# A decoder step on one core: modulation tiles placed one by one, the mLSTM update behind the numerator, and the RWKV-7 preparation split by columns

## What is computed

```python
mod = (jax.nn.silu(c) @ p['w_ada'] + p['b_ada'])[:, None, :]
sh_a, sc_a, g_a, sh_c, sc_c, g_c = jnp.split(mod, 6, axis=-1)
h = rmsnorm(x, p['norm_mix_g']) * (1.0 + sc_a) + sh_a
z = h @ p['w_in']
y_a, new_shift, new_wkv = rwkv7_mix(z_a, shift_s[l], wkv_s[l], p)
y_b, new_conv, new_C, new_n, new_m = mlstm_mix(z_qk, z_rest, conv_s[l], C_s[l], n_s[l], m_s[l], p)
y_mix = jnp.concatenate([y_a, y_b], axis=-1).astype(x.dtype) @ p['w_out']
x = x + g_a * y_mix
h = rmsnorm(x, p['norm_ffn_g']) * (1.0 + sc_c) + sh_c
x = x + g_c * peer_ffn(h, p['peer_wq'], p['peer_keys'], p['peer_u'], p['peer_v'])
```

## Time and profile before

| | |
|---|---|
| median of three runs | 3084.05 us (3083.44 to 3085.71) |
| profiled execution | 3082.83 us |
| its span | 3081.0 us |
| PE / DVE / ACT / POOL busy | 91 / 41 / 32 / 57 % |
| mean granted PE clock | 0.933 |
| transfers | 544.5 MB, 177 GB/s in the mean |

### The profile page before, as it was taken

The page is one execution under the profiler, slowest core; times in us unless marked ns, Lnnn a source line. Parts: engine busy times, 40 slices in busy tenths (PEclk is TensorE's granted clock), DMA queues, the critical chain, the costliest instruction groups (busy, mean ns, idle before and its releaser), DMA issues.

```text
span 3081.0 us, 57118 instructions
## 1 busy us (share of the span) xinstructions
PE 2797.0 (91%) x23015; PEld 2579.8 (84%) x23015; DVE 1265.1 (41%) x2180; ACT 989.4 (32%) x1358; POOL 1756.2 (57%) x722
## 2 busy tenths in 40 slices
PE   5689998979875979998999999899999899999997
PEld 1389996637653979998999899899999899989997
DVE  0350654372226640895788713200131201463233
ACT  1243432132102233444344332233333233223323
POOL 0167771012211757688455477677777677777674
PEclk9699998669885989999999999999999999999999
DMA  9534446866672334344344444455444455444442
GB/s 354 219 140 166 157 165 210 313 249 220 229 284 84 148 111 164 129 159 161 136 174 168 148 164 157 151 186 188 164 154 169 164 187 194 159 160 164 151 164 99
DMA packets 153351, 544.49 MB, mean 177 GB/s; under 512 B 9080, under 2 KB 22024, under 8 KB 124168
## 3 DMA queue, kind: packets, MB, share of 16 engines
q1 hardware_dynamic: 136384, 505.18, 45.2%
q10 hardware_dynamic: 14680, 20.43, 1.9%
q0 software_dynamic: 2160, 17.03, 1.3%
HBM read 518.76 MB, written 23.84 MB: 176 GB/s over the span
## 4 chain that ended last, share of the span: by engine, by line
issue 33%; POOL 29%; PE 28%; DVE 6%; DMA 4%; ACT 1%; POOLq 0%; SPq 0%; ACTq 0%; DVEq 0%
POOL ring_lo L579 29%; PE bank L652 27%; DMA kept<-in_w_ada 3%; DVE staged L1622 1%; DMA kept<-in_w_adaf 1%; DVE staged L1567 1%; DVE staged L1905 1%; DVE staged L1894 0%; ACT hi_front L1217 0%; ACT staged L1217 0%; DMA out_n_all<-staged 0%; DVE staged L1581 0%; PE bank L655 0%; POOLq L578 0%; DVE staged L1785 0%
## 5 line engine op out<-in xcount | busy, mean ns | idle before, releaser
L579 POOL TENSOR_TENSOR ring_lo<-kept,hi_peer 128x1024 fp32r<-128x1024 f32 x576 | 1444.7, 2529 | 614.4 <-ACT hi_peer L1217 614.4
L1217 ACT ACTIVATE hi_peer<-kept 128x1024 fp32r<-128x1024 f32 x576 | 578.2, 1052 | 1224.5 <-PE bank L652 1224.3
L652 PE MATMUL bank<-h_hi,ring_lo 128*128 128x288 f32 x3104 | 918.1, 296 | 0.0
L652 PE MATMUL bank<-h_hi,hi_peer 128*128 128x288 f32 x2304 | 690.0, 299 | 36.9 <-DVE staged L1905 16.0
L652 PE MATMUL bank<-h_lo,hi_peer 128*128 128x288 f32 x2304 | 683.8, 297 | 0.0
L652 PE MATMUL bank<-act_hi,hi_peer 128*128 128x288 f32 x2048 | 615.1, 300 | 35.3 <-DVE act_lo L2033 15.5
L652 PE MATMUL bank<-act_lo,hi_peer 128*128 128x288 f32 x2048 | 609.5, 298 | 0.0
L652 PE MATMUL bank<-act_hi,ring_lo 128*128 128x288 f32 x2048 | 609.3, 298 | 0.0
L652 PEld LDWEIGHTS bank<-h_hi,ring_lo 128*128 128x128 f32 x3104 | 588.6, 190 | 0.0
L652 PEld LDWEIGHTS bank<-h_hi,hi_peer 128*128 128x128 f32 x2304 | 436.1, 189 | 40.2 <-issue 35.7
L652 PE MATMUL bank<-staged 64*64 64x64 f32 (+13 forms) x5488 | 377.3, 276 | 89.8 <-issue 20.3
(11 more groups left out here) (187 smaller groups left out, 2452.3 us busy)
## 6 DMA issues: line engine op xcount, KB each, us to landing
kept<-in_peer_u SPq DMA_DIRECT2D x128, 1024.0 KB, 4.7
kept<-in_peer_v SPq DMA_DIRECT2D x128, 1024.0 KB, 5.5
kept<-in_w_ada SPq DMA_DIRECT2D x96, 1024.0 KB, 8.8
kept<-in_w_in SPq DMA_DIRECT2D x50, 1024.0 KB, 4.7
kept<-in_w_adaf SPq DMA_DIRECT2D x32, 1024.0 KB, 9.1
kept<-in_w_out SPq DMA_DIRECT2D x16, 1024.0 KB, 4.8
kept<-in_w_q SPq DMA_DIRECT2D x16, 1024.0 KB, 4.8
gates_spill<-staged ACTq DMA_DIRECT2D x32, 432.0 KB, 2.7
```

The costliest lines, as they stand in the source:

```text
L579: pool.tensor_tensor(ring_lo[:, n % RING_SLOTS, cols], ring[n % RING_SLOTS][:, cols], hi_slot(n)[:, cols].bitcast(F32), ALU.subtract).then ...
L652: return pe.matmul(out, lhsT, rhs, start=start, stop=stop)
L1217: return act.activation(out, in_, ACT.Copy)
```

## The change

Every `ada_more(n)` now stands for n single tiles and not n quarters, and there are more calls, some of them ahead of the heads; ACT follows the same list of places.

```diff
-            def ada_quarter(j, quarter):
+            def ada_step(j, quarter, q):
...
-                for q in range(4):
-                    n = ada_tile(j, quarter) + q
-                    arrived(pe, n)
-                    for g in range(4):
-                        mm = matmul(out[32 * g:32 * g + 32, :], silc[:, 4 * q + g, :],
-                                    ring[n % RING_SLOTS][:, g * 512:(g + 1) * 512], q == 0, q == 3)
-                    mm.then_inc(used, 1)
+                n = ada_tile(j, quarter) + q
+                arrived(pe, n)
+                for g in range(4):
+                    mm = matmul(out[32 * g:32 * g + 32, :], silc[:, 4 * q + g, :],
+                                ring[n % RING_SLOTS][:, g * 512:(g + 1) * 512], q == 0, q == 3)
+                mm.then_inc(used, 1)
```

Ahead of the heads: one tile after every second of eight broadcasts and after every third of nine turns. In the heads, PE:

```diff
             pe.wait_ge(S("turn_done"), 9)
-            for h in range(BH):
-                if h >= 1:
-                    pe.wait_ge(S("ms_root"), h)
+            def scores(h):
...
-                ada_more(1)
+            scores(0)
+            for h in range(BH):
                 pe.wait_ge(S("s_ready"), h + 1)
                 pe.wait_ge(S(f"c_landed{h % 2}"), 16 * (h // 2 + 1))
+                if h:
+                    pe.wait_ge(S("num_used"), h)
...
                 mm.then_inc(S("num_ready"), 1)
-                ada_more(1)
-                pe.wait_ge(S("hsq_ready"), h + 1)
-                pe.wait_ge(S("num_used"), h + 1)
-                for i in range(2):
-                    mm = matmul(ps[0][:, 0:N], ones, hsq[:, i, :], i == 0, i == 1)
-                mm.then_inc(S("ms_ready"), 1)
...
+                if h:
+                    pe.wait_ge(S("ms_root"), h)
+                    pe.wait_ge(S("upd_used"), h * NS)
                 for u in range(NS):
-                    if u >= 3 or h > 0:
-                        pe.wait_ge(S("upd_used"), h * NS + u - 2)
-                    out = ps[1 + u % 3][:, 0:DV + 1]
+                    if u >= 2:
+                        pe.wait_ge(S("upd_used"), h * NS + u - 1)
+                    out = ps[4 + u % 2][:, 0:DV + 1]
...
-                pe.wait_ge(S("upd_used"), (h + 1) * NS)
-            ada_more(1)
+                    if u in (1, 4):
+                        ada_more(2 if u == 1 else 1)
+                if h + 1 < BH:
+                    scores(h + 1)
+                ada_more(1)
+                pe.wait_ge(S("hsq_ready"), h + 1)
+                pe.wait_ge(S("upd_used"), h * NS + NS - 1)
+                for i in range(2):
+                    mm = matmul(ps[5][:, 0:N], ones, hsq[:, i, :], i == 0, i == 1)
+                mm.then_inc(S("ms_ready"), 1)
+                ada_more(3)
+            ada_more(3)
```

DVE's order in a head is now: reciprocal and numerators of h, decays of h + 1, nine updates of h, scores of h + 1, then the normalisation of h. ACT squares h, makes the exponentials of h + 1, then the root of h. POOL's stores and ACT's waits:

```diff
             def store_c(h):
-                pool.wait_ge(S("c_new"), h + 1)
+                pool.wait_ge(S("upd_used"), (h + 1) * NS)
...
-            pool.dma_start(T["n_all"], n_out).then_inc(S("small_stored"), 16)
-            pool.wait_ge(S("small_stored"), 64)
+            pool.dma_start(T["n_all"], n_out).then_inc(S("n_stored"), 16)
+            pool.wait_ge(S("n_stored"), 16)
```

Preparation: ACT makes the root of kk's sums ahead of the eight identities; DVE makes the inverse norm right behind the scans, ahead of the logs. The exponential that k and B need goes to a tile `kd` of its own. The operands are made for the first 128 columns only, the other 160 in the first pair:

```diff
-            tt(ar[:, :, 1, :], r, ar[:, :, 1, :], ALU.mult)
-            tt(Bf, Bf, lgf, ALU.mult).then_inc(S("ops_ready"), 1)
-            dve.wait_ge(S("rk_made"), 1)
-            tt(kf, kf, lgf, ALU.mult).then_inc(S("ops_ready"), 1)
+            def operand(step, cols):
+                if step == 0:
+                    tt(ar[:, :, 1, cols], r[:, :, cols], ar[:, :, 1, cols], ALU.mult)
+                elif step == 1:
+                    tt(B[:, :, cols], B[:, :, cols], kd[:, :, cols], ALU.mult).then_inc(S("ops_ready"), 1)
+                else:
+                    tt(kd[:, :, cols], k[:, :, cols], kd[:, :, cols], ALU.mult).then_inc(S("ops_ready"), 1)
+            for step in range(3):
+                dve.wait_ge(S("decays_ready"), min(step + 2, 3))
+                operand(step, slice(0, P))
...
+                if p == 0:
+                    operand(0, slice(P, N))
                 for i in range(1, LEVELS):
...
+                    if p == 0 and i < 3:
+                        operand(i, slice(P, N))
```

Bonus: POOL's products of r and k stand behind the masks of levels 3 and 4 of the first pair, that with a_rk behind the last mask, PE's eight sums and ACT's copies in levels 2 to 5 of the second pair, and the product by v in the sample part, ahead of `vm`:

```diff
+                    if p == 0 and (i == 3 or i == 4):
+                        half = slice(4 * (i - 3), 4 * (i - 3) + 4)
+                        pool.wait_ge(S("ops_ready"), 4)
+                        pool.tensor_tensor(k[:, half], r[:, half], k[:, half], ALU.mult).then_inc(S("rk_made"), 1)
+                if p == 0:
+                    pool.wait_ge(S("rk_made"), 2)
+                    pool.tensor_tensor(k, k, over(prm("rk"), 2, N), ALU.mult).then_inc(S("rk_ready"), 1)
...
+            pool.wait_ge(S("rk_taken"), MT)
+            pool.tensor_tensor(kf, kf, vf, ALU.mult).then_inc(S("bonus_ready"), 1)
```

More of the change, by code:

```diff
@@ L909, in _ @@
                         times(q, q, mk[i % 2], Ti).then_inc(S("x_sum"), 1)
+                    if p == 1 and i >= 2:
+                        if i == 2:
+                            pe.wait_ge(S("rk_ready"), 1)
+                            pe.wait_ge(S("akv_done"), 2 * (p + 1))
+                        for e in range(2):
+                            f = 2 * (i - 2) + e
+                            if f >= 2:
+                                pe.wait_ge(S("rk_taken"), f - 1)
+                            matmul(ps[4 + e][:, 0:N], blk, k[:, f, :]).then_inc(S("rk_sum"), 1)
+                    ada_more(1)
                     for q in range(2):
@@ L1253, in _ @@
             pending = [(j, q) for j in range(2, 8) for q in range(4)]
+            ada_steps = [0]
             def ada_more(count):
-                for _ in range(min(count, len(pending))):
+                assert ada_places[len(ada_steps) - 1] == count
+                ada_steps.append(min(ada_steps[-1] + count, 96))
+                while 24 - len(pending) < ada_steps[-1] // 4:
                     j, q = pending.pop(0)
-                    if (j, q) == (2, 0):
-                        continue
-                    if q == 1 and j > 2:
+                    if q == 0 and j > 2:
                         ada_store(j - 1)
-                    ada_take(*((j, q - 1) if q else (j - 1, 3)))
+                    ada_take(j, q)
             def hi(n, i=0):
@@ L1373, in _, with decays @@
                 copy(bc[:, u // BH, u % BH, :], ps[2 + u % 2][:, 0:N]).then_inc(S("bc_done"), 1)
-            for h in range(BH):
+                if u % 2:
+                    ada_more(1)
+            for _ in range(3):
                 ada_more(1)
+            def decays(h):
                 act.wait_ge(S("d_ready"), h + 1)
@@ L1704, in _, with decays @@
             n0 = aux("n0", BH, NB)
-            for h in range(BH):
-                if h:
-                    dve.wait_ge(S("c_new"), h)
+            def decays(h):
                 mx = bc[:, 0, h, :]
@@ L1723, in _ @@
                 tt(dd[0:SM, 1, TP + P:DW], ps[0][0:SM, TP + P:DW], dd[0:SM, 0, TP + P:DW], ALU.mult).then_inc(S("s_ready"), 1)
+            decays(0)
+            scores(0)
+            for h in range(BH):
                 dve.wait_ge(S("num_ready"), h + 1)
+                if h:
+                    dve.wait_ge(S("c_new"), h)
                 link(stt(out=rec[:, 0, :], in0=ps[3][:, 0:N], scalar=-1.0, in1=bc[:, 1, h, :], op0=ALU.mult, op1=ALU.max))
@@ L1729, in _ @@
                 tt(hh[:, 1, :], ps[2][:, 0:N], rec[:, 0, :], ALU.mult).then_inc(S("num_used"), 1)
+                if h + 1 < BH:
+                    decays(h + 1)
                 if h >= 2:
```

184 lines of the change are left out of this document (98 added, 86 removed).

## The result

The changed kernel takes 3053.5 us (median of 4 runs, 3049.1 to 3060.0) against 3084.5 for the kernel before (4 runs beside it): ratio 0.9899, 95% interval 0.9882 to 0.9915. That is 31 us faster, of 39 forecast. The profiled execution took 3050.79 us (span 3049.0), 32.0 us less than the one of before. Single runs of the changed kernel lie up to 11 us apart, so two kernels that differ by 5 us are told apart here only by the lengths of stages. A stage wanders too: over the six profiles (this one, e0, e2, e5, e6, e7) with the same code in and behind the heads, the stage up to the low-rank sum took 148.1 to 155.1 us, and the unchanged code behind the first w_out matmul took 2079.2 to 2086.3 us over all profiles.

The account below looks back on a forecast made before the run. TensorE was taken as busy 2797 of 3081 us, with only 479 to 1001.6 us touched; the terms 6.5 - 1 - 7.4 - 4.1 - 30.4 - 3 + 0 sum to -39.4, so 3043.4, 3045 for the median, range 3022 to 3068.

Parts of the forecast that it names:

- Parts 5 and 6: RWKV pairs: single tiles end transfer waits and cold stretches at their ends (-30.4 us) and fill gaps inside (-3).
- three places: First pair's end: tiles of three places stand almost back to back in the kernel before (768.77 to 787 us).
- The three operand pieces: Remaining 160 columns of three operands on DVE in the first pair, 1.4 us each; each could wait for a GpSimd mask.
- Part 4: RWKV preparation: B x kk without GpSimd's product -3.4, two products cut to 128 columns -2.8, root moved ahead +2; -4.1 us.
- Part 1: Broadcasts and turns ahead of the heads: seven tiles added at 8.5 us, some 2 hidden; +6.5 us.
- Part 2: mLSTM heads: five tiles fewer -6.1, idle time gone -5.0, waits for DVE +6.4, two banks +4; -1 us, bounds -20 and +20.
- DVE's pace is 0.52 us for an update: Updates in the heads: DVE's time for one, taken from a 0.47 us row with a small one between.
- The wait of 1.6 us a head: Behind each head's numerator: PE waits for DVE's operations and decays before the updates, four times, +6.4 us.
- The 1 us a head for two banks: Updates in the heads: round trips over two banks instead of three add perhaps 0.15 x 7 us a head, +4 in all.
- Rival 2: Cold heads: all 28 tiles there at 1.94 us, 20 us more, 3065 us; chance 0.15.
- Part 3: Behind the heads: ScalarE's wait for the store of n, and PE's 7.4 us behind it, go; -7.4 us.
- Part 7: Sample part: five more tiles, 6 us, hidden in PE's idle time; 0 us (-2 to +4).

Follow-up runs that it names:

- e0: The changed kernel run again unedited, as the yardstick of its group: 3059.3 us (6 runs), ratio 0.9907 to the kernel before.
- e2: The changed kernel with GpSimd's sample-part product by v moved behind vm and the issue of the wkv_p store: 3062.1 us, ratio 0.9917.
- e5: The changed kernel with the columns split undone, the preparation making its operands for all 288 columns: 3064.5 us, ratio 0.9931.
- e6: The changed kernel with ScalarE's wait for the store of n put back ahead of its sigmoids: 3060.8 us, ratio 0.9904.
- e7: The changed kernel with the 41 tiles of the pairs in groups of four again: 3064.4 us, ratio 0.9939.
- e3: The changed kernel with the updates of C going round three banks instead of two: 3054.1 us, ratio 0.9894.
- e4: The changed kernel with each head's four tiles together between the numerator and the updates: 3045.0 us, ratio 0.9863.
- e8: The changed kernel with the heads' old order and three banks, no tiles behind the heads, one tile less in the sample part: 3052.7 us, ratio 0.9893.
- e1: The changed kernel with the three tiles behind the heads moved into the group norm's first three steps: 3038.2 us, ratio 0.9844.
- e12: e10 with the sample part's bonus product moved from GpSimd to VectorE: 3038.1 us, ratio 0.9849, on another chip than e10.
- e10: The changed kernel with the edits of e1 and e4 together: 3035.7 us (5 runs), ratio 0.9831.

## Why the prediction was right, and where not

**Faster, inside the range, by the parts that were to carry it.** Parts 5 and 6 were to give 33.4 of 39.4 us and gave 38.7. The transfer waits are gone as forecast (the prediction's "three places" between 768.77 and 787 us are two quarters, which its sum had right). More than forecast came from the clock: 0.98 in the first pair, and the grams behind its end take 1.98 us a group, where I had taken only 3 us off for all that stood cold behind the stall. That the transfer waits would go was the mechanism, and they went; how the 38.7 us divide between waits, clock and gaps is not shown beyond e7's 4 to 8.5. The three operand pieces in the first pair took 1.49 us each, as priced, and none was held. But two of them met an idle GpSimd, and where one did overlap a mask, the mask was held by it (3.09 instead of 2.36 us):

```profile
704.46 1.49 DVE L1856 TENSOR_TENSOR staged<-staged 128x1280 f32<-128x1280 f32 x1
705.06 3.09 POOL L621 TENSOR_TENSOR staged<-staged 128x1024 f32<-128x1024 f32 x1 [7.41 <-DVE staged L1880]
```

Part 4 (4.1, measured 4.4) was sized right, and both its terms are shown (e5). Part 1 (6.5, measured 6.1) came out right by two errors: the seven tiles took 10.7 us and not 8.5, since four of them ran wholly or in part at the low clock, and hid some 4.6 us of waits and not 2.

**Part 2 failed in one term: "DVE's pace is 0.52 us for an update".** That is the pace while PE's clock is high. Behind the numerator PE's clock was at 0.50, for the first two updates of every head and for all of them in two heads of four (three in e0, four in e3), and there the two records of an update take 1.03 us: PE sets the pace, and the updates cost 11.9 us more. The wait of 1.6 us a head that I had put in their place is not there. The 1 us a head for two banks was hidden where the clock was low (e3) and is real where it is high: e4 takes 11.5 of e0's 31.2 us back, and its two updates take 1.40 us where DVE's pace would give 1.04. e8, with the old order and three banks, has updates of 17.3 us, at the high clock for the most part. Up to the last head's sum of squares the changed kernel took 128.9 us with 25 tiles, the kernel before 127.8 with 32: what the seven tiles gave back went into the slower updates. Rival 2 had the right cause, cold heads, but put its 20 us on the heads' fillers; all 96 together grew by 4.4 us (120.9 against 116.5); the bill came to the small matmuls. What I said would show part 2 wrong (a stage under 120 or over 160 us) was too wide to catch it: 148.1 us to the low-rank sum.

The rule of the Trainium skill weighed there (TensorE: Matmul & The Clock Gate, "A second HAM failure mode: psum-queue depth-cycling") puts a falling clock down to small gaps between groups of matmuls. These traces do not bear it out as the cause here: in the last head the updates ran at the low clock with no gaps, and in e4, with gaps of 0.18 to 0.34 us before every second update, at the high one.

**Part 3 failed in "-7.4".** The wait for n's store did go, but e6 shows that it was no longer worth anything: six tiles in place of four, a transfer wait of 3.6 us and a turn of 7.0 us (5.2 before) stand on PE ahead of the low-rank sum, 19.2 us against 18.0 with the wait. I had counted the tiles at 1.21 us each, had no term for a transfer wait in that place, and had not asked what arrives last once the store's wait is gone. e1 takes three of the tiles, the transfer wait and the turn away, and its stage is 18.2 us shorter.

**Part 7 failed by 5.8 us.** By the two timelines: tokens and their copies 1.5, three tiles at the low clock 1.0 more than four at the high one, the sums by levels 1.0, the middle three tiles 2.6 (5.05 us in a gap of 2). The last three tiles do stand inside DVE's wait, as forecast. The 1.5 us come from DVE's copy, which took 7.81 us beside two GpSimd products. The Trainium skill (SBUF — State Buffer, "SBUF: two separate sides") calls the pair of ports that DVE and GpSimd share an exclusive lock, held for a whole instruction. The trace agrees in that the copy ends when a product ends (872.54 and 872.44 us, and with one product 854.03 and 853.94 in e12); that it was not let in between the two products goes beyond what the page says. In the first pair, where I had expected it, it was GpSimd that was held.

The summed forecast erred by less than its parts because the pairs' surplus (5.3), the norm's 2.3 us and 1.3 us in code that did not change paid for part of the heads and of the sample part. That is luck. What stays open: whether e10 is truly faster than e1; what the order of the heads is worth by itself; and why the clock comes up behind the first tiles in some heads and not in others. The last moves the heads' stage by some 4 us a time from one execution to the next (148.1 us with two cold heads, 152.2 with three), so the 2 us by which e1's stage gained more than the 16.6 us of wait, turn and tiles that left it need no cause of their own.

## What to carry to other kernels

A duration read at the high clock is not the price of the same work in another place: for work that is moved, look at the granted clock and at what PE did just before its new place, and ask which engine sets the pace at either level. A filler costs little where it fills a wait, and may even pay by keeping PE warm for what follows (e4, and the group norm's first sums); it costs its whole length, and the transfer wait and turn behind it, where the next engine waits for PE. When a wait is counted as gained, name what arrives last in its place.

## What the runs showed of the hardware that I had not expected

- 32-row matmuls of 257 columns took 1.03 us an update (two records) at the low clock with PE never idle, and 0.57 to 0.61 behind four 128x512 tiles, with nothing changed but the place of these tiles (28.7 or 31.2 us for 64 records against 19.7).
- At the high clock two engines that pass work over two PSUM banks left each other idle, 0.18 and 0.27 us in each 1.40, where three banks held 0.52 us an update (17.3 and 16.8 us for 64 records against 19.7 and 2.7 of waits).
- A VectorE copy of 128 x 128 elements took 7.81 us beside two GpSimd products in a row, 3.82, 2.80 and 2.69 beside one, and a product of that size 5.26 instead of 0.28 us. In the other direction a GpSimd mask took 3.09 instead of 2.36 us beside a VectorE product.
- The same store of n landed 10.2 us behind its issue in the kernel before and 5.0 to 5.2 us in six profiles after the change.
- Single runs of one program spread by 7 to 20 us (e3: 3043.6 to 3063.4), those of e1 by 2 us.
